# A one-core trunk with experts: a limit on how many expert weight loads are under way

## The chip, the cores and the metric

The kernel runs on one core of one Trainium2 chip. The metric is the device time of one execution in microseconds (us); lower is better. The core has engines with instruction queues of their own: PE (matrix products, with its weight loads shown as PEld), DVE, ACT, POOL, and SP, which here does nothing but wait and issue DMAs. The core's 16 DMA engines move all data between HBM and the on-chip memory.

## The reference

Two layers of a decoder trunk over 288 tokens (256 prompt tokens and 8 sequences of 4 tokens), width 1024, all in float32. Each layer is a token mixer (three recurrent branches) and a feed-forward part. The second layer's feed-forward part is what matters here: eight experts, of which each token takes the two with the highest router logits.

```python
def swiglu(h, w1, w3, w2):
    return (jax.nn.silu(h @ w1) * (h @ w3)) @ w2

def moe_swiglu(h, router, w1, w3, w2):
    logits = (h @ router).astype(jnp.float32)
    top_v, top_i = lax.top_k(logits, TOP_K)
    probs = jax.nn.softmax(top_v, axis=-1)
    gate = jnp.sum(jax.nn.one_hot(top_i, N_EXPERTS, dtype=jnp.float32) * probs[..., None], axis=-2)
    out = jnp.zeros(h.shape, jnp.float32)
    for e in range(N_EXPERTS):
        out = out + gate[..., e:e + 1] * swiglu(h, w1[e], w3[e], w2[e]).astype(jnp.float32)
    return out.astype(h.dtype)
```

w1 and w3 are 1024 x 2816 for each expert, w2 is 2816 x 1024.

## The kernel before

The program does layer 0 (mixer and dense feed-forward), then the mixer of layer 1, then the experts (function `experts`, L2489). Weights never stay on the chip: they come as **slabs** of 128 x 1024 float32, 512 KB each. An expert has 66 slabs (`EX_SLABS`): 44 for w1 and w3 in turn (`UP_SLABS`), 22 for w2. One **pass** is one expert's work on the tokens gathered for it: 88 columns of tokens in the first two passes, then 80, 80, 76, 76 and 72, 72. With these inputs there are eight passes.

PE does a pass in `expert` (L2674): 44 times `up` (L2621; its matmuls are L2630), then the gathering for the next pass (L2602, L2608), then eight times `down` (L2642; matmuls L2650) with the adding of the result to the tokens (`add_up` L2665, `to_tokens` L2672) between. PE's two halves of a weight block are separate matmuls, and the trace has 32 matmul records for a slab, each with a weight load beside it. The passes are loops of PE's own queue (`pe.Fori`), two passes to a loop, with the pass's code written out once in each.

The slabs land in a **ring of 22 places** (`EX_RING`), made of buffers whose data is no longer needed: 2 places in lora_w, 2 in hT, 2 in y_ret, 6 in proj, 8 in ring, 2 in merged, used in this order. Slab n of a pass takes place n % 22, and as 66 is three times 22 each pass begins at place 0. Two neighbouring places are a pair and share a semaphore (`pair_in`); a load adds 16 to it when it has landed. PE waits in `pair_here` (L2613) for both slabs of a pair before it uses the first. After a slab's last matmul PE adds 1 to `slab_done`.

SP issues the loads in the order of use. The first 22 are issued during the mixer's end (`ahead`, L2170). All others go through `load` (L2533): SP waits until `slab_done` says that the slab 22 places earlier has been used (L2534), and issues the load (L2535). Slabs 22 to 65 of the first pass are written out (L2537); the seven further passes are a loop of SP, which reads the expert's number from memory at its start (L2542) and then issues 66 loads (L2543). Nothing else limits how many loads are under way at a time: it is whatever PE's pace of freeing places makes it.

`settle` is an increment of a semaphore that nobody waits for.

Of the kernel before, what the change touches and what calls it, by code (L numbers as in the profile page):

```python
# [55 lines left out]
EX_RING = 22  # L56
# [7 lines left out]
STREAM = ((3, 8), (GLA_H, 6), (GLA_H, 6), (KT, 4), (2, 8), (1, 8))  # L64
# [23 lines left out]
def fills(p, place):  # L88

    return sum(g for g, n in STREAM[:p] if place < n)  # L90
# [8 lines left out]
EX_SLABS = UP_SLABS + EX_DOWN  # L99
# [125 lines left out]
def build(nc, xT_in, w_mix, w_lora, w_rank, w_gkup, vec_in, vecf_in, router_in, w_ff, s_ret, s_gla, s_rw,  # L225
# [50 lines left out]
    def settle(eng):  # L276


        eng.sem_inc(settled, 1)
# [81 lines left out]
    def slabs_in(buffer, n):  # L361
# [3 lines left out]
    EX_AT_LORA, EX_AT_HT, EX_AT_Y, EX_AT_PROJ, EX_AT_RING, EX_AT_MERGED = 0, 2, 4, 6, 12, 20  # L365
    pair_in = {s: slab_in[s - EX_AT_RING] if EX_AT_RING <= s < EX_AT_MERGED else nc.alloc_semaphore(name=f"pair_in{s}")
               for s in range(0, EX_RING, 2)}
# [14 lines left out]
    def slabs_before(layer, p):  # L382

        return layer * (MIX_SLABS + FF_SLABS) + BASE[p]

    def fills_before(layer, s):

        return layer * (fills(len(STREAM), s) + len(range(s, FF_SLABS, RING)))
# [241 lines left out]
    def half(ap, h):  # L630
        return ap[64 * h:64 * h + 64]
# [737 lines left out]
    def rwkv(nc, block, sig, layer, joined):  # L1369
# [33 lines left out]
            "p (g s) -> p g s", g=2)[:, :, 0:GT]  # L1403
        TILES = (0, 0), (1, 1), (0, 1), (1, 0)
        nlev = len(LEVELS64) - 1
# [18 lines left out]
        def group(g):  # L1424
            return slice(NP + GT * g, NP + GT * g + GT)

        def window(g, first=0):
            return slice(NP + GT * g - first, NP + GT * g - first + CH)
# [31 lines left out]
        def _(pe):  # L1460
# [37 lines left out]
            def scores(i):  # L1498
# [6 lines left out]
                for n, src in enumerate((bt, kt)):  # L1505
                    for cp in range(2):
                        for h, r in TILES:
                            c = 2 * cp + r
# [4 lines left out]
            def scores_rest(i):  # L1513
# [5 lines left out]
                for cp in range(2):  # L1519
                    for h, r in TILES:  # L1520
                        c = 2 * cp + r
                        mm(unit(half(BY_HEAD2[h], 1 - r), cp), unit(half(at_rt, h)[:, 0], c), unit(half(bt, h), c),
                           start=True, stop=True)
                for cp in range(2):
                    for h, r in TILES:
                        c = 2 * cp + r
                        mm(unit(half(BY_HEAD3[h], 1 - r), cp), unit(half(bt, h), c), unit(half(at_rt, h)[:, 0], c),
                           start=True, stop=True)
                for h, g in TILES:
                    mm(half(BY_HEAD2[h], 1 - g)[:, 2 * CH:2 * CH + GT], half(at_rt, h)[:, 0, window(g)],  # L1530
                       half(bt, h)[:, group(g)], start=True, stop=True)
                for h, g in TILES:
                    mm(half(BY_HEAD3[h], 1 - g)[:, 2 * CH:2 * CH + GT], half(bt, h)[:, window(g)],
# [955 lines left out]
    def experts(nc, block, sig, layer, merge, rs):  # L2489
# [24 lines left out]
        OTOK, ADD = (bank[6], bank[4]), (bank[7], bank[5])  # L2514
        FF0 = slabs_before(layer, len(STREAM))
        TILES = ((0, 128), (128, 128), (256, 32))

        def passes(eng):
            eng.wait_ge(sig("ctl"), 1)
            return eng.value_load(ctl[0:1, ENTRIES:ENTRIES + 1], min_val=NE - FIXED, max_val=MAXR)  # L2520

        def count(p, per, k):

            i, done = p
            return i * per + (done * per + k)
# [4 lines left out]

        @block.sync
        def _(sp):
            def load(p, e, n):  # L2533
                sp.wait_ge(slab_done, count(p, EX_SLABS, FF0 + n - EX_RING + 1))  # L2534
                sp.dma_start(ex_slot[n % EX_RING], w_ff[e, n]).then_inc(pair_in[n % EX_RING // 2 * 2], 16)  # L2535

            for n in range(EX_RING, EX_SLABS):  # L2537
                load((0, 0), 1, n)
            sp.wait_ge(sig("ctl"), 1)
            after_first = sp.value_load(ctl[0:1, ENTRIES + 1:ENTRIES + 2], min_val=NE - 1, max_val=FIXED - 1 + MAXR)  # L2540
            with sp.Fori(0, after_first) as i:
                e = sp.value_load(ctl[0:1, bass.ds(i, 1)], min_val=0, max_val=NE)  # L2542
                for n in range(EX_SLABS):  # L2543
                    load((i, 1), e, n)
            for k in range(0, KT, 2):
                sp.wait_ge(sig("normed"), k + 2)
                sp.dma_start(yT_out[:, k:k + 2, :], hT[:, k:k + 2, :]).then_inc(sig("stored"), 16)
            sp.wait_ge(sig("stored"), 4 * 16)
# [646 lines left out]
    for layer in range(DEPTH):  # L3195
        with phase(nc, f"in{layer}") as (block, projected):
            project_in(nc, block, projected, layer)
            retained = Signals(nc, f"ret{layer}")
            retention(nc, block, retained, layer, projected)
            gated_linear(nc, block, Signals(nc, f"gla{layer}"), layer, retained)  # L3200
        with phase(nc, f"rw{layer}") as (block, delta):
            joined = Signals(nc, f"join{layer}")
            rwkv(nc, block, delta, layer, joined)
            merge = Signals(nc, f"mix{layer}")
            rs = mix_out(nc, block, merge, layer, delta, joined)
            if layer > 0:
                experts(nc, block, Signals(nc, "moe"), layer, merge, rs)
# [98 lines left out]
```

## Time and profile before

| what | us |
|---|---|
| median of 3 runs (lowest, highest) | 2607.95 (2605.93, 2608.48) |
| the profiled execution, its own time | 2606.82 |
| its span, first to last instruction | 2605.0 |
| the eight passes of the experts, within the span | 1769 to 2590 |

The span is 1.8 us shorter than the profiled execution's own time, and that execution is 1.1 us below the median. A page of the profile gives the busy time of each engine and the share of the DMA engines in 40 slices of the span; the experts are the last 13 of them. From there one goes to the table by stretches (one row a pass), to who waited for whom, to PE's and SP's own instructions in order of time, and to the DMA queues with the time from a load's issue to its landing. In the timelines a row gathers neighbouring instructions of one kind: start, length, engine, line, what is written and read, count, and in brackets the idle time before it with what ended it. "issue" there means that the engine waited for nothing that the profile shows.

### The profile page before, as it was taken

How to read it: one execution, taken by the hardware profiler on the slowest of the kernel's cores; microseconds unless marked ns; L12 is line 12 of the kernel's file. 1: busy time of each engine (PE TensorE's matmuls, PEld its weight loads, DVE VectorE, ACT ScalarE, POOL GpSimd, SP SyncE). 2: the span in 40 equal slices, each digit the busy share in tenths (PEclk: the TensorE clock that was granted, in tenths of full speed). 3: DMA queues.
4: the chain of work that ended last, by engine and by line, in shares of the span. 5: the costliest groups of instructions: out<-in, count | busy, mean ns of one | idle time of the engine just before them, and what ended most of it. 6: DMA issues, size and time to landing. Idle time of an engine off the chain costs nothing. (4 is left out here: it accounts for less than half of the span.)

```text
span 2605.0 us, 103336 instructions
## 1 busy us (share of the span) xinstructions
PE 2437.4 (94%) x45930; PEld 2038.3 (78%) x45930; DVE 1287.5 (49%) x3333; ACT 606.7 (23%) x1798; POOL 0.2 (0%) x4
## 2 busy tenths in 40 slices
PE   9999999999999999999999999999899888878878
PEld 8987666666889998987666666788888787777767
DVE  7666666666786766666666666773111111111111
ACT  2233323333211102233333343211111101111101
POOL 0000000000000000000000000000000000000000
PEclk9999999999999999999999999999999999999989
DMA  6334432222334443334433222367899899999984
GB/s 240 107 139 162 157 131 81 76 76 86 133 131 153 176 147 119 136 131 156 151 122 97 76 80 81 132 238 299 289 348 353 327 355 339 345 340 347 340 301 158
DMA packets 142766, 498.59 MB, mean 191 GB/s; under 512 B 18401, under 2 KB 23137, under 8 KB 139905
## 3 DMA queue, kind: packets, MB, share of 16 engines
q1 hardware_dynamic: 142336, 492.24, 52.5%
q8 instruction: 346, 5.67, 0.8%
q14 instruction: 84, 0.68, 0.1%
HBM read 471.88 MB, written 20.29 MB: 189 GB/s over the span
## 5 line engine op out<-in xcount | busy, mean ns | idle before, releaser
L305 PE MATMUL psum<-hT,ring 128*64 128x144 f32 (+1 forms) x4568 | 457.0, 345 | 3.9 <-DVE hT L2450 1.7
L305 PEld LDWEIGHTS psum<-hT,ring 128*64 128x64 f32 x4568 | 291.7, 137 | 97.7 <-issue 12.2
L2952 DVE TENSOR_TENSOR work<-psum,work 128x88 f32<-128x88 f32 (+3 forms) x176 | 42.4, 241 | 459.5 <-PE psum L2630 459.3
L2630 PE MATMUL psum<-work,ring 128*64 128x88 f32 (+3 forms) x4096 | 157.2, 237 | 35.7 <-issue 35.5
L1782 ACT ACTIVATE work<-psum 128x256 f32<-128x256 f32 (+4 forms) x320 | 103.9, 362 | 349.9 <-PE psum L1693 84.8
L2630 PEld LDWEIGHTS psum<-work,ring 128*64 128x64 f32 x4096 | 151.6, 141 | 39.8 <-issue 39.8
L305 PE MATMUL psum<-work 128*64 128x144 f32 (+4 forms) x2096 | 154.8, 282 | 4.3 <-DVE work L1273 3.6
L305 PE MATMUL psum<-y_ret,work 128*64 128x144 f32 x2400 | 156.2, 286 | 1.2 <-DVE y_ret L546 1.2
L2734 ACT ACTIVATE work<-psum 128x88 f32<-128x88 f32 (+3 forms) x176 | 41.7, 237 | 472.4 <-PE psum L2630 468.8
L305 PEld LDWEIGHTS psum<-y_ret,work 128*64 128x64 f32 x2400 | 148.7, 137 | 1.4 <-issue 1.4
L305 PEld LDWEIGHTS psum<-work 128*64 128x64 f32 (+2 forms) x2096 | 122.0, 136 | 30.7 <-issue 11.4
L2943 DVE TENSOR_TENSOR xT<-xT,psum 128x288 f32<-128x288 f32 x64 | 29.1, 454 | 231.9 <-PE psum L2665 230.9
L2630 PE MATMUL psum<-work,proj 128*64 128x88 f32 (+3 forms) x3072 | 113.8, 231 | 22.2 <-issue 22.1
L305 PE MATMUL psum<-y_ret,ring 128*64 128x144 f32 (+1 forms) x1280 | 127.2, 332 | 2.5 <-ACT work L1782 2.5
L2630 PEld LDWEIGHTS psum<-work,proj 128*64 128x64 f32 x3072 | 109.3, 136 | 25.1 <-issue 25.1
L305 PEld LDWEIGHTS psum<-y_ret,ring 128*64 128x64 f32 x1280 | 79.9, 137 | 18.4 <-ACT work L1782 4.5
L2650 PE MATMUL psum<-work,ring 128*64 128x88 f32 (+3 forms) x2048 | 76.3, 231 | 8.3 <-issue 8.3
L2650 PEld LDWEIGHTS psum<-work,ring 128*64 128x64 f32 x2048 | 72.8, 136 | 11.2 <-issue 11.2
L327 PE MATMUL psum<-hT,ring 128*128 128x288 f32 x252 | 72.8, 408 | 0.0
L2630 PE MATMUL psum<-work,lora_w 128*64 128x88 f32 (+3 forms) x1024 | 46.6, 254 | 27.7 <-issue 27.6
L1578 PEld LDWEIGHTS psum<-work 64*64 64x64 f32 x1408 | 47.3, 134 | 29.4 <-issue 17.7
L305 PE MATMUL psum<-hT,work 128*64 128x144 f32 x928 | 69.1, 287 | 0.0
(538 smaller groups left out, 4389.7 us busy)
## 6 DMA issues: line engine op xcount, KB each, us to landing
ring<-w_mix_dram SPq DMA_DIRECT2D x256, 512.0 KB, 4.1
ring<-w_ff_dram SPq DMA_DIRECT2D x256, 512.0 KB, 5.3
proj<-w_ff_dram SPq DMA_DIRECT2D x144, 512.0 KB, 6.2
lora_w<-w_ff_dram SPq DMA_DIRECT2D x48, 512.0 KB, 4.7
hT<-w_ff_dram SPq DMA_DIRECT2D x48, 512.0 KB, 5.7
y_ret<-w_ff_dram SPq DMA_DIRECT2D x48, 512.0 KB, 6.3
merged<-w_ff_dram SPq DMA_DIRECT2D x48, 512.0 KB, 5.7
work<-s_gla_dram SPq DMA_DIRECT2D x8, 1024.0 KB, 5.1
```

Source lines behind the costliest of these rows:

```text
L305: last = nc.tensor.matmul(out[64 * c:64 * c + 64], weights[:, 64 * c:64 * c + 64], x, start=start, stop=stop)
L327: mm = (in_halves if self.narrow else nc.tensor.matmul)(out, ring[:, s, k, :], rhs[:, k, :], start=(k == 0), stop=(k == KT - 1))
L1578: last = mm(unit(half(W, r), c), half(AT, 1 - r)[:, c], half(X, 1 - r)[:, c], start=True, stop=True)
L1782: return nc.scalar.activation(out, in_, func, **kw)
L2630: last = mm(bank[n % 4][64 * h:64 * h + 64, 0:cap], ex_slot[n % EX_RING][:, k, 64 * h:64 * h + 64], hg[:, k, 0:cap], start=(k == 0), stop= ...
L2650: last = mm(DOWN[m % 2][64 * h:64 * h + 64, 0:cap], ex_slot[(UP_SLABS + n) % EX_RING][:, k, 64 * h:64 * h + 64], hid[:, f, 0:cap], start=( ...
L2734: ac(act1[:, f % 2, 0:cap], bank[2 * f % 4][:, 0:cap], ACT.Silu).then_inc(sig("w1_free"), 1)
L2943: tt(xT[:, k, :], xT[:, k, :], ADD[m % 2][:, 0:T], ALU.add).then_inc(sig("added"), 1)
L2952: tt(hid[:, f, 0:cap], bank[(2 * f + 1) % 4][:, 0:cap], act1[:, f % 2, 0:cap], ALU.mult).then_inc(sig("w3_free"), 1)
```

## The change

`load` gets one more wait ahead of its old one. For the first slab of each pair SP now waits until both slabs of the pair two ahead of it have landed: slab n waits for slabs n - 4 and n - 3 (`UNDER_WAY` is 4). In the loop the first two pairs of a pass wait for the last two pairs of the pass before. The new function `landed` works out the semaphore and its value as `pair_here` does for PE. When a pair is issued, only the pair ahead of it may be under way, so after the second slab's issue there are four at most, and three after the first slab's. Ahead of every load SP also executes one `settle`. The old wait on `slab_done`, the order of the loads, the places, and every instruction of the other engines stay as they are.

```diff
@@ -2514,6 +2514,7 @@
         TILES = ((0, 128), (128, 128), (256, 32))
+        UNDER_WAY = 4
@@ -2530,7 +2531,21 @@
         @block.sync
         def _(sp):
+            def landed(p, n):
+
+                s = n % EX_RING
+                earlier = 0
+                if EX_AT_RING <= s < EX_AT_MERGED:
+                    earlier = fills_before(layer, s - EX_AT_RING) + fills(len(STREAM), s - EX_AT_RING)
+                sp.wait_ge(pair_in[s], count(p, EX_SLABS // EX_RING * 32, earlier * 16 + (n // EX_RING + 1) * 32))
+
             def load(p, e, n):
+                i, done = p
+                if n % 2 == 0 and n >= UNDER_WAY:
+                    landed(p, n - UNDER_WAY)
+                elif n % 2 == 0 and done:
+                    landed((i, done - 1), n - UNDER_WAY + EX_SLABS)
+                settle(sp)
                 sp.wait_ge(slab_done, count(p, EX_SLABS, FF0 + n - EX_RING + 1))
                 sp.dma_start(ex_slot[n % EX_RING], w_ff[e, n]).then_inc(pair_in[n % EX_RING // 2 * 2], 16)
```

What stands in SP's queue before, in the written-out part of the first pass, is below, with the semaphores that each group of loads waits for (`slab_done` alone):

```order
L2535 DMA ring<-w_ff_dram 128x1024 [waits slab_done] x8
L2535 DMA merged<-w_ff_dram 128x1024 [waits slab_done] x2
L2535 DMA lora_w<-w_ff_dram 128x1024 [waits slab_done] x2
L2535 DMA hT<-w_ff_dram 128x1024 [waits slab_done] x2
L2535 DMA y_ret<-w_ff_dram 128x1024 [waits slab_done] x2
```

In the changed kernel the same place of SP's queue reads so (the line of the load is now L2550; pair_in8 and pair_in10 are the last pairs of proj, slab_in0 to slab_in6 the four pairs of ring):

```order
L2550 DMA ring<-w_ff_dram 128x1024 [waits pair_in8,slab_done]
L2550 DMA ring<-w_ff_dram 128x1024 [waits slab_done]
L2550 DMA ring<-w_ff_dram 128x1024 [waits pair_in10,slab_done]
L2550 DMA ring<-w_ff_dram 128x1024 [waits slab_done]
L2550 DMA ring<-w_ff_dram 128x1024 [waits slab_in0,slab_done]
L2550 DMA ring<-w_ff_dram 128x1024 [waits slab_done]
L2550 DMA ring<-w_ff_dram 128x1024 [waits slab_in2,slab_done]
L2550 DMA ring<-w_ff_dram 128x1024 [waits slab_done]
L2550 DMA merged<-w_ff_dram 128x1024 [waits slab_in4,slab_done]
L2550 DMA merged<-w_ff_dram 128x1024 [waits slab_done]
```

No load has moved; every second one has a second semaphore to wait for.

## Rows read from the trace of the kernel before

**Rows 1.** The page: engines' busy time, and DMA share in 40 slices.
```profile
PE 2437.4 (94%) x45930; PEld 2038.3 (78%) x45930; DVE 1287.5 (49%) x3333; ACT 606.7 (23%) x1798; POOL 0.2 (0%) x4
...
DMA  6334432222334443334433222367899899999984
```

**Rows 2.** Table by stretches, five of the eight passes; columns in the first line.
```profile
core 0: us, PE busy (x) PEld busy (x) DVE busy (x) ACT busy (x) POOL busy (x), PEclk, DMA share, GB/s
1769.00:1874.00 105.00, 93.97 (x2243) 88.55 (x2243) 20.20 (x82) 11.96 (x41) 0.00 (x0) 0.99 0.90 333
...
2181.00:2287.00 106.00, 82.64 (x2243) 77.57 (x2243) 13.23 (x43) 13.37 (x44) 0.00 (x0) 0.99 0.92 343
2287.00:2386.00 99.00, 83.12 (x2248) 78.25 (x2245) 12.96 (x42) 10.37 (x40) 0.00 (x0) 0.99 0.92 342
...
2493.00:2590.00 97.00, 82.65 (x2227) 78.40 (x2225) 11.70 (x39) 9.79 (x38) 0.00 (x0) 0.92 0.65 241
```

**Rows 3.** Who waited for whom, 1769 to 2590: total us, times, longest.
```profile
PE psum L2630 <- issue: 106.7, 69, 5.7
...
PE psum L2650 <- issue: 16.3, 22, 2.1
```

**Rows 4.** PE's timeline, from the second pass.
```profile
1917.29 6.91 PE L2630 MATMUL psum<-work,proj 128*64 128x88 f32 x174 [1.49 <-issue]
...
1928.16 5.07 PE L2630 MATMUL psum<-work,ring 128*64 128x88 f32 x126 [0.89 <-issue]
1934.17 2.22 PE L2630 MATMUL psum<-work,ring 128*64 128x88 f32 x52 [0.93 <-issue]
1936.16 2.68 PE L2630 MATMUL psum<-work,merged 128*64 128x88 f32 x64
```

**Rows 5.** SP's queue, 1700 to 2600: what its waits ended on.
```profile
SPq L2535 <- PE psum L2630: 356.5, 348, 16.6
SPq L2535 <- PE psum L2650: 115.0, 123, 3.6
```

**Rows 6.** SP's timeline: the first loads of L2535.
```profile
1770.96 1.56 SPq L2535 DMA_DIRECT2D lora_w<-w_ff_dram  x2
```

**Rows 7.** SP's timeline, some loads of the second pass.
```profile
1906.46 1.56 SPq L2535 DMA_DIRECT2D merged<-w_ff_dram  x2
...
1937.81 1.84 SPq L2535 DMA_DIRECT2D merged<-w_ff_dram  x2
1946.04 1.49 SPq L2535 DMA_DIRECT2D lora_w<-w_ff_dram  x2
1947.82 0.91 SPq L2535 DMA_DIRECT2D hT<-w_ff_dram  x2
```

**Rows 8.** Queues, and issues with median us to landing, 1769 to 2590.
```profile
q8 instruction: 149, 2.44, 1.1%
...
ring<-w_ff_dram SPq DMA_DIRECT2D x184, 512.0 KB, 5.6
proj<-w_ff_dram SPq DMA_DIRECT2D x138, 512.0 KB, 6.2
lora_w<-w_ff_dram SPq DMA_DIRECT2D x46, 512.0 KB, 4.6
```

**Rows 9.** Loads of L2535, 1800 to 2500.
```profile
DMA to landing us min/median/max: 3.1/5.7/8.8
```

**Rows 10.** A stretch of dense loading; columns as in rows 2.
```profile
1950.00:2000.00 50.00, 46.98 (x1131) 43.52 (x1129) 8.12 (x23) 6.94 (x25) 0.00 (x0) 1.00 0.97 354
```

**Rows 11.** DMA, 1887 to 1901.
```profile
DMA packets 1498, 5.48 MB, mean 391 GB/s; under 512 B 168, under 2 KB 168, under 8 KB 1495
```

**Rows 12.** PE's timeline at the end of the last pass.
```profile
2570.65 5.17 PE L2650 MATMUL psum<-work,proj 128*64 128x72 f32 x160
...
2587.61 2.17 PE L2650 MATMUL psum<-work,merged 128*64 128x72 f32 x64
```

**Rows 13.** DMA queues, 2562 to 2590.
```profile
q8 instruction: 7, 0.11, 1.7%
```

## The prediction, written before the changed kernel ran

> **What bounds the kernel now.** I read the page first. PE is busy 94% of the span, and the DMA engines, a third to half busy before, are at nine tenths in the last third, where the experts are [rows 1]. The change touches only that part, so I split it by passes. A pass takes 97 to 107 us, and DMA is at 0.90 to 0.92 of its time until the last pass, whose loads end early [rows 2]. PE's busy time falls with the token columns, from 94 us (88 columns) to 83 (76 and 72), yet the passes hardly get shorter. So something paces PE. The list of waits shows it: PE's matmuls waited 106.7 us (69 times) in `up` and 16.3 us (22 times) in `down`, for "issue", nothing that the profile names [rows 3]. That is 123 us in 91 waits, 1.35 us each. Every other engine's long waits are for PE.
>
> Are these waits for weights? No. SP's waits all end on PE's `slab_done` [rows 5]: each load is issued as soon as its place is free. The pair issued into merged at 1906.5 [rows 7] lands some 6 us later (the median is 5.7 [rows 9]), and PE first reads those places at 1936.2 [rows 4]. Weights lie 24 us ahead of PE.
>
> The waits come after about 127 matmuls or a multiple of it: 1917.29 begins 174 of one group, another 79 follow in ring (253 in all, a wait at 1928.16), then 126, then a wait [rows 4]. 127 matmuls with their 127 weight loads are about 256 instructions. Queue q8 fetched 149 packets of instructions, 2.44 MB, so 16 KB each, in these 821 us: one in 5.5 us [rows 8]. So I take the waits for **PE waiting for its own instructions**, which come over the DMA engines that carry the weights. The end of the last pass supports it: with no load left, q8 still brings 7 packets in 28 us [rows 13], one in 4 us, and PE does 160 matmuls in 5.17 us without a wait [rows 12], 4.1 us for 128. With loads under way a fetch must take longer than the 4.1 to 5.1 us that 126 to 128 matmuls last.
>
> So two clocks run. PE's side: its work and the fetches, which get slower with what is queued for DMA. The supply side: 506 loads (184 + 138 + 4 x 46 [rows 8]), one in 1.57 us over the 794 us from 1771 [rows 6] to about 2565. Now the supply is slaved to PE; loads under way are 5.7 / 1.57 = 3.6 on average.
>
> **The change, part by part.** *The new wait.* It holds SP, whose queue has nothing but the following loads behind it; PE is the one who would wait, and only once the 24 us of lead are used up. Peaks go: two loads can be issued within 0.6 us (0.91 us for two whose own issue is 0.33 [rows 7]), and the longest landing, 8.8 us, against 3.1 for the shortest [rows 9], means several loads ahead; now never more than three. On average I expect 3.2 under way in place of 3.6 (four after a pair's issue, two before the next).
>
> *What PE gains.* A fetch at 1928 took 5.1 + 0.9 = 6.0 us from one wait's end to the next [rows 4]; without loads it takes at most 4.1 [rows 12]. That is at least (6.0 - 4.1) / 3.6 = 0.5 us for each load under way. 0.4 loads less and no peaks: I take 0.4 us off each of the 91 waits, 36 us. Bounds: 0.15 us (14 us), if only the average counts and less than linearly, and 0.6 us (55 us), if the peaks make the waits. PE's side alone then ends the span at 2605 - 36 = 2569, between 2550 and 2591.
>
> *What the supply can do.* Two pairs go per round trip of a pair: if SP reacts in 0.3 us and the second load is issued 0.6 us behind the first, a median landing of 5.7 us makes a round of 6.6 us for four loads, 1.65 us each. That bound assumes that landings do not get shorter, though they now queue behind fewer. With 5.4 it is 1.575. From below the engines bound it: 391 GB/s in a dense stretch [rows 11] is 524288 B / 391 = 1.34 us a load; the shortest landing, 3.1 us, would allow less than that. I take the row of a long dense stretch, share 0.97 and 354 GB/s [rows 10]: 1.48 us. At the start of SP's loop body there is a hole (1939.65 to 1946.04, 6.4 us [rows 7], where a pair is due each 3.0): 3.4 us lost, seven times, 24 us. Last issue: 1771 + 506 x 1.48 + 24 = 2544. It lands 4.8 us later, at 2549; PE needs 2.2 us for its pair and 15.2 us more to the span's end (2589.8 to 2605.0 [rows 12]): 2566. So the lead of 24 us is spent in the course of the passes, and both sides end near each other. The later one, 2569, and 1 us for where they meet give 2570.
>
> *`settle` and the wait themselves.* An increment on a queue that waits for PE or for landings anyway; SP issues no faster than one load in 0.6 us when it may and needs one in 1.48, so they cost nothing while that cover of 0.9 us holds. If SP's longer code made its hole at the loop's start 1 us longer, it would be 7 us in all.
>
> *The other engines.* Nothing moves. DVE and ACT follow PE.
>
> **A rule against it.** What the trace shows is a fetch of 6.0 us beside loads, 4.1 at most without [rows 4, 12]. The Trainium skill, "DMA: Bandwidth & Descriptors", in "Queues, rings and completion order", says that each DMA engine goes round its queues packet by packet. By that rule an instruction fetch waits for a packet or so of the weights, not for all that is queued, and 3 or 6 loads under way are the same to it; that is rival A. By my reading of the rows it waits for the backlog.
>
> **The rivals.**
> *A. The depth does not matter.* Fetches are slow because the engines are busy at all, at 0.90 and more [rows 2]. Then PE keeps its pace of 5.5 us a fetch and the supply, at less than 1.57 us a load, stays slaved to PE. For it: the demand stays the same. Against it: landings spread from 3.1 to 8.8 us, so queues do matter to whatever lies in them. Time: as before, 2607.
> *B. The supply starves PE (slower).* If a load takes more than 1.56 us with this limit, the lead runs out and PE waits at `pair_here`. The price: 506 us for each us of the load's time. At 1.65, the sum above with unchanged landings, the last issue is 1771 + 835 + 24 = 2630, the end 2652, plus 2 for the time outside the span: 2654. At 1.575 it is 2592 + 22 = 2614, or 2616. It decides from 1.557 us a load, where the sum 1771 + 24 + 22.2 + 506 x (the last landing, PE's pair and the tail are the 22.2) gives 2605. For it: the median landing. Against: that median includes queueing behind up to six loads, which the limit removes, and DMA had stretches of 391 GB/s.
> *C. The limit seldom holds.* SP would find the pair landed. With landings of 5.7 us and issues each 1.23 to 1.5 us the pair two ahead is normally still under way at an issue, so I give it little: 2607.
>
> **How the numbers follow.** The forecast (both sides improve, 2550 to 2600): 0.54. A and C: 0.16, within a few us of 2607; of that I count 0.02 as faster, 0.11 as the same and 0.03 as slower. B: 0.30; about half of it lies at loads of 1.555 to 1.58 us, that is 2604 to 2617 (0.03 of it no different from now), the rest above. The span of 2570 with 1.8 us outside it is 2572, and the median lies 1.1 us above the profiled execution: 2573. The low end is PE's best bound, 2550. The high end is 2622, between B's two prices, which leaves out some 0.15 above and 0.05 below. Faster than 2602.7, which is 0.2%, about what a measurement of this kernel can tell from no change: 0.54 + 0.02 = 0.56. Within 0.2%: 0.11 + 0.03 = 0.14. Slower: 0.03 + 0.27 = 0.30.
>
> **What would show it.** Right: PE's waits for "issue" in `up` fall from 1.5 us each to about 1.1, to some 85 us in all; the median landing falls to about 5 us and the longest below 7; SP's waits end on landings; the lead of loads over PE shrinks to a few us in the last passes, and DMA's share is no lower. A shows as the old waits with a new landing median. B shows as PE's matmuls waiting with landings as their releasers, at the first slab of a pair, and a DMA share that falls below 0.85. Wrong altogether would be the guess on the instructions: then the 91 waits stay whatever the landings do.

## The result: slower by 0.6%

| | us |
|---|---|
| changed kernel, median of 3 runs (lowest, highest) | 2624.77 (2620.37, 2627.01) |
| kernel before, the same | 2607.95 (2605.93, 2608.48) |
| ratio, 95% interval | 1.0064 (1.0041 to 1.0086) |
| the changed kernel's profiled span | 2623.0 |

The forecast was 2573, in a range of 2550 to 2622. Rival B of the prediction had it: the supply of weights starves PE.

SP's queue first. Who ended its waits, 1700 to 2620, with total us, times and longest (L279 is the line of the increment that follows the new wait, L2550 the load):

```profile
SPq L279 <- DMA ring<-w_ff_dram: 162.7, 91, 4.2
SPq L279 <- DMA proj<-w_ff_dram: 134.1, 69, 3.5
SPq L279 <- DMA hT<-w_ff_dram: 44.4, 23, 4.4
SPq L279 <- DMA y_ret<-w_ff_dram: 43.6, 23, 3.5
SPq L279 <- DMA merged<-w_ff_dram: 42.9, 22, 4.1
SPq L279 <- DMA lora_w<-w_ff_dram: 40.2, 23, 3.3
...
SPq L2550 <- PE psum L2645: 21.5, 15, 13.8
```

Before, all 471 waits ended on PE's `slab_done` [rows 5]. Now 251 end on landings, and 506 loads are 253 pairs: the limit holds at practically every pair, and the ring's free places no longer say anything. SP's timeline shows the beat that results (start, length, then the issue):

```profile
1915.28 0.99 SPq L2550 DMA_DIRECT2D merged<-w_ff_dram  x2
1918.85 0.99 SPq L2550 DMA_DIRECT2D lora_w<-w_ff_dram  x2
1922.48 0.99 SPq L2550 DMA_DIRECT2D hT<-w_ff_dram  x2
1925.99 0.99 SPq L2550 DMA_DIRECT2D y_ret<-w_ff_dram  x2
...
1950.64 0.99 SPq L2550 DMA_DIRECT2D merged<-w_ff_dram  x2
1953.97 1.00 SPq L2550 DMA_DIRECT2D lora_w<-w_ff_dram  x2
...
2597.03 1.84 SPq L2550 DMA_DIRECT2D merged<-w_ff_dram  x2
```

The 506 loads are issued from 1773.0 to 2597.7: 1.63 us a load, where before (1771.0 to 2560.4) it was 1.56 with the issues slaved to PE. A single load lands sooner, over 1800 to 2520:

```profile
DMA to landing us min/median/max: 3.4/4.9/8.5
```

against a median of 5.7 [rows 9]. But the next pair is not issued on a single load's landing. It waits for a whole pair. From the issues and landings of the trace, a pair takes 6.26 us from its first issue to its second landing (mean): the second load is issued 0.65 us behind the first and lands 5.6 us after its own issue, the first one 4.4 us after its own. SP reacts in 0.28 us, and two pairs go per round: (6.26 + 0.28) / 4 = 1.635 us a load.

The first seven passes of the changed kernel (the columns are in the first line):

```profile
core 0: us, PE busy (x) PEld busy (x) DVE busy (x) ACT busy (x) POOL busy (x), PEclk, DMA share, GB/s
1772.00:1875.00 103.00, 92.47 (x2233) 87.97 (x2231) 19.35 (x76) 11.96 (x41) 0.00 (x0) 1.00 0.89 317
1875.00:1974.00 99.00, 94.85 (x2245) 90.46 (x2245) 13.57 (x42) 10.63 (x40) 0.00 (x0) 0.95 0.91 323
1974.00:2072.00 98.00, 84.57 (x2231) 79.23 (x2227) 13.09 (x41) 13.08 (x43) 0.00 (x0) 0.98 0.91 323
2072.00:2175.00 103.00, 90.38 (x2237) 83.49 (x2239) 13.13 (x42) 10.40 (x40) 0.00 (x0) 0.97 0.90 326
2175.00:2288.00 113.00, 85.22 (x2235) 77.43 (x2235) 12.87 (x41) 13.01 (x43) 0.00 (x0) 1.00 0.89 318
2288.00:2393.00 105.00, 87.13 (x2235) 81.12 (x2235) 12.96 (x42) 10.37 (x40) 0.00 (x0) 0.96 0.90 323
2393.00:2506.00 113.00, 84.70 (x2241) 77.33 (x2243) 12.63 (x41) 12.85 (x42) 0.00 (x0) 0.97 0.91 324
```

Put beside [rows 2] and the passes between them, there are two halves. The first three passes take 300.5 us where before they took 311.8: 11 us **faster**. The other five take 535.3 where it was 508.5: 27 us **slower**. With 2 us more before the first pass and 0.5 us at the end that is the 18 us between the spans.

The turn comes where the lead is gone. The lead is the time from a pair's landing to PE's first use of it. In steps of 22 slabs, at the places in merged, it is in us:

```text
before:   22 28 30 23 27 25 21 27 29 24 26 26 22 26 28 21 26 23 24 26 31 23 22
changed:  15 20 21 12 14  9  0  0  3  0  0  0  0  0  0  0  0  0  0  0  1  0  2
```

Three of these numbers are a pass; the first pass has two, as its first 22 slabs were issued ahead. From the end of the third pass on the lead is zero but for a few us here and there, and PE waits for weights, as the list of its waits over 1773 to 2608 says:

```profile
PE psum L2645 <- issue: 51.6, 31, 6.3
PE psum L2645 <- DMA ring<-w_ff_dram: 24.3, 24, 3.1
PE psum L2645 <- DMA proj<-w_ff_dram: 13.3, 14, 2.6
PE psum L2645 <- DMA merged<-w_ff_dram: 7.6, 7, 2.6
PE psum L2665 <- issue: 7.5, 10, 1.7
PE psum L2665 <- DMA ring<-w_ff_dram: 6.4, 7, 1.9
```

(L2645 and L2665 are the matmuls of `up` and `down`, L2630 and L2650 before.) The waits for "issue" halve, from 123 us [rows 3] to 59. Waits for landings, which did not exist, take their place with some 70 us, counting the smaller rows. Together the waits are 7 us longer than before; PE's busy time is 12 us longer (2449.0 against 2437.4 [rows 1]), 8 of them within the eight passes. PE's weight loads that wait beside running matmuls can be in it, and so can the granted clock of 0.988 in place of 0.990; how the 12 us divide is not measured. One stretch of the sixth pass shows the pattern, a wait at every other pair or so, each ended by a landing:

```profile
2339.17 2.33 PE L2645 MATMUL psum<-work,ring 128*64 128x76 f32 x64 [1.72 <-DMA ring<-w_ff_dram]
2341.66 2.33 PE L2645 MATMUL psum<-work,ring 128*64 128x76 f32 x64 [0.16 <-DMA ring<-w_ff_dram]
2345.49 2.33 PE L2645 MATMUL psum<-work,ring 128*64 128x76 f32 x64 [1.51 <-DMA ring<-w_ff_dram]
2348.00 2.33 PE L2645 MATMUL psum<-work,ring 128*64 128x76 f32 x64 [0.17 <-DMA ring<-w_ff_dram]
2352.90 2.33 PE L2645 MATMUL psum<-work,merged 128*64 128x76 f32 x64 [2.58 <-DMA merged<-w_ff_dram]
```

### The profile page after: what moved, and what is told of

It is laid out like the page before. It is cut to its first block and busy times, and to the rows that moved or that the text cites. A ratio compares the mean times of both kernels' runs of the same rounds, so it can differ in the third digit from the quotient of the medians.

```text
span 2623.0 us, 103933 instructions
## 1 busy us (share of the span) xinstructions
PE 2449.0 (93%) x45930; PEld 2043.3 (78%) x45930; DVE 1287.2 (49%) x3333; ACT 606.8 (23%) x1798; POOL 0.2 (0%) x4
## 5 line engine op out<-in xcount | busy, mean ns | idle before, releaser
L2645 PE MATMUL psum<-work,ring 128*64 128x88 f32 (+3 forms) x4096 | 154.2, 234 | 36.6 <-DMA ring<-w_ff_dram 24.3
L2645 PEld LDWEIGHTS psum<-work,ring 128*64 128x64 f32 x4096 | 147.6, 138 | 42.2 <-issue 42.2
L2645 PE MATMUL psum<-work,proj 128*64 128x88 f32 (+3 forms) x3072 | 116.9, 235 | 22.3 <-DMA proj<-w_ff_dram 13.3
L2645 PEld LDWEIGHTS psum<-work,proj 128*64 128x64 f32 x3072 | 112.1, 139 | 26.0 <-issue 25.9
L2665 PE MATMUL psum<-work,ring 128*64 128x88 f32 (+3 forms) x2048 | 76.1, 232 | 8.4 <-DMA ring<-w_ff_dram 6.4
L2665 PEld LDWEIGHTS psum<-work,ring 128*64 128x64 f32 x2048 | 72.3, 136 | 11.7 <-DMA ring<-w_ff_dram 8.2
L2645 PE MATMUL psum<-work,lora_w 128*64 128x88 f32 (+3 forms) x1024 | 47.0, 258 | 29.9 <-issue 25.6
L2645 PEld LDWEIGHTS psum<-work,lora_w 128*64 128x64 f32 x1024 | 44.1, 158 | 33.0 <-issue 33.0
```

Of the source, the lines that this page charges most:

```text
L2645: last = mm(bank[n % 4][64 * h:64 * h + 64, 0:cap], ex_slot[n % EX_RING][:, k, 64 * h:64 * h + 64], hg[:, k, 0:cap], start=(k == 0), stop= ...
L2665: last = mm(DOWN[m % 2][64 * h:64 * h + 64, 0:cap], ex_slot[(UP_SLABS + n) % EX_RING][:, k, 64 * h:64 * h + 64], hid[:, f, 0:cap], start=( ...
```

## The experiments

Theory T: the limit sets the supply at two pairs per round trip, 1.63 us a load, PE wants less, and the lead of 24 us is spent in about three passes; after that PE runs at the pace of the supply. Beside it stands theory I of the prediction: PE's waits for "issue" are instruction fetches that the weights on the DMA engines hold up. Rivals were that SP's added instructions cost, and that any wait on a landing costs. Times are medians, the ratios are to the kernel before on the same chip; e4, e6, e7 and e8 ran once each.

### Is it the increment, or any limit?

In e1 the waits go and the increment ahead of every load stays:

```diff
-                if n % 2 == 0 and n >= UNDER_WAY:
-                    landed(p, n - UNDER_WAY)
-                elif n % 2 == 0 and done:
-                    landed((i, done - 1), n - UNDER_WAY + EX_SLABS)
                 settle(sp)
```

> The changed kernel without the waits on landings; the added increment ahead of every load stays. Theory T (four under way are too few: a pair's round trip sets the supply at 1.63 us a load): the increment costs nothing, the kernel is back at the time of before, 2605 to 2611 us, median landing 5.7 us. Rival S (SP's added instructions slow its issues): most of the loss stays, 2618 us or more.

2601.48 us, ratio 0.9980 (0.9968 to 0.9993). The loss is gone; rival S falls. The time lies under the expected 2605 to 2611: that the increment alone would make the kernel 0.2% faster was not expected, and I have no explanation for it. It matters below as a yardstick.

In e2 and e3 the limit stays and is wider, six and eight:

```diff
-        UNDER_WAY = 4
+        UNDER_WAY = 6
```

> UNDER_WAY 6: a pair waits for the pair three ahead, five or six loads under way at most. Theory T: three pairs for each round trip of some 7 us give 1.17 us a load, more than the DMA engines can do, so the supply is no longer the limit; the wait holds SP only at the peaks. The time is that of before or a little less, 2595 to 2608 us, landings 5.5 us in the median and none above 8. Rival L (any wait on a landing costs, by SP's reaction and by stopping the stream): slower than before, 2613 us or more.

2601.69 us, ratio 0.9985 (0.9974 to 0.9997), landings 3.1/5.7/8.2 from 1800 to 2500 (shortest, median, longest; a little over the expected 8).

> UNDER_WAY 8: seven or eight at most. Before had rarely more than six under way, so theory T says 2603 to 2610 us, no different from before. Rival L (any wait on a landing costs): 2613 us or more.

2603.21 us, ratio 0.9998 (0.9985 to 1.0010). In e3 SP waited for a landing only once, so it says nothing of such waits; it is in effect e1 again, and the 0.9980 there beside the 0.9998 here shows how far two such ratios can lie apart. In e2 SP waited for landings 74 times, 49 us in all, and the kernel was no slower: a wait on a landing costs nothing by itself, and rival L falls. Nor does cutting the peaks help: with six, 3 loads of 449 took over 7.5 us to land, before 19 of 443, and PE's waits were the same as with the increment alone. Two rows each of PE's waits, 1769 to 2610, of e1 (L2641, L2661) and then of e2:

```profile
PE psum L2641 <- issue: 101.0, 68, 5.9
PE psum L2661 <- issue: 15.2, 18, 1.9
```

```profile
PE psum L2645 <- issue: 101.8, 71, 5.8
PE psum L2665 <- issue: 15.2, 19, 1.7
```

### Does the round trip set the supply?

e4 sets `UNDER_WAY` to 2, so that one pair is under way at a time.

> UNDER_WAY 2: a pair waits for the pair ahead of it, so one pair under way. Theory T: the supply is one pair in a round trip of some 4.6 us (3.1 us shortest landing, 0.65 us for the second issue, 0.3 us reaction, 0.5 us for the queue) or 2.3 us a load: 506 loads take 1164 us instead of 825, the kernel 2960 us, between 2900 and 3050. Rival B2 (the engines' rate, not the round trip, limits the changed kernel): much less than proportional, under 2750 us. Waits of PE for instructions: if they come from the loads queued, those outside the waits for loads fall to a few us in all.

3191.68 us, so rival B2, the engines' rate, falls. Its SP timeline:

```profile
2004.64 0.99 SPq L2550 DMA_DIRECT2D merged<-w_ff_dram  x2
2010.09 0.99 SPq L2550 DMA_DIRECT2D lora_w<-w_ff_dram  x2
2015.72 0.99 SPq L2550 DMA_DIRECT2D hT<-w_ff_dram  x2
2021.52 0.99 SPq L2550 DMA_DIRECT2D y_ret<-w_ff_dram  x2
```

A pair each 5.54 us in the mean, which is the pair's round trip in this run, 5.26 us, and the reaction of 0.28: 2.77 us a load. The law holds in both kernels: pairs allowed, divided by a pair's round trip and SP's reaction. I had the round trip itself too short (4.6 us), by taking a landing of 3.1 us for both loads; so the time missed the expected 2900 to 3050. Waits for "issue" in `up` were 17.3 us in all here, more than the few us expected, beside 491 us of waits for landings.

e5 moves the wait from the pair's first load to its second, so that five are under way at the peak and a round is one load's landing instead of a pair's:

```diff
-                if n % 2 == 0 and n >= UNDER_WAY:
+                if n % 2 == 1 and n >= UNDER_WAY:
                     landed(p, n - UNDER_WAY)
-                elif n % 2 == 0 and done:
+                elif n % 2 == 1 and done:
```

with `UNDER_WAY = 5`.

> The wait stands ahead of a pair's second load, on the pair two ahead of it: four loads under way after that load, five after the next pair's first. Four loads now go per round trip of one load (about 5.2 us and 0.3 us reaction) in place of a pair's (6.5 us). Theory T (the round trip over four loads sets the supply): 1.38 us a load, below PE's need of 1.55, so PE no longer waits for loads and the time is 2598 to 2610 us. Rival (the engines' rate falls with any limit): PE still waits for landings, 2613 us or more.

2602.61 us, ratio 0.9991 (0.9979 to 1.0002). One more load under way, and PE waits for no landing any more, while SP still waits for 72 landings in ring and 69 in proj. The threshold lies between four by pairs and this limit of five. The median landing was 5.4 us and PE's waits for "issue" 115.8 us (97.8 in `up`, 18.0 in `down`), much as in e1.

### Are the waits for "issue" fetches held up by the weights?

e6 and e7 are the kernel before with smaller loads: half and an eighth of each slab. They leave out the rest of the weights, and PE multiplies with what lies there; its instructions are the same.

```diff
-                sp.dma_start(ex_slot[n % EX_RING], w_ff[e, n]).then_inc(pair_in[n % EX_RING // 2 * 2], 16)
+                sp.dma_start(ex_slot[n % EX_RING][:, 0:4], w_ff[e, n][:, 0:4]).then_inc(pair_in[n % EX_RING // 2 * 2], 16)
```

(`0:1` in e7.)

> The kernel before, in which each load of the experts' loop and of the first pass after its first 22 brings only half of a slab (256 KB), so the products use stale weights in the other half. PE's instructions are the same. Theory I (PE's waits for issue are instruction fetches held up by the weights on the DMA engines): with DMA at half its share the waits of 117 us fall to under 40 us and the time to 2500 to 2540 us. Rival P (the waits belong to PE's own instruction stream whatever DMA does): they stay at 100 us or more, 2590 us or more.

2489.49 us, some 10 us under the expected range. PE's waits for "issue" in `up`, 1769 to 2480, and the landings:

```profile
PE psum L2630 <- issue: 32.1, 27, 4.4
```

```profile
DMA to landing us min/median/max: 2.5/3.3/5.2
```

> As the half loads, but an eighth of a slab (64 KB), so DMA is nearly idle and the products use stale weights for the rest. Theory I: the waits for issue between matmuls are gone but for those at the loop's jumps (four of up to 5 us), under 25 us in all, the time 2485 to 2515 us. Rival P: 100 us of waits or more, 2590 us or more.

2466.98 us, again under the range, and of the waits only seven in `up` are left, four of them over 3 us:

```profile
PE psum L2630 <- issue: 17.2, 7, 3.5
```

With DMA at a fifth of its share the passes at last follow the token columns:

```profile
1769.00:1865.00 96.00, 91.14 (x2236) 87.10 (x2235) 19.98 (x80) 11.95 (x41) 0.00 (x0) 1.00 0.18 49
...
2294.00:2372.00 78.00, 75.13 (x2235) 71.42 (x2235) 12.71 (x42) 12.85 (x42) 0.00 (x0) 0.99 0.22 60
```

PE's waits come from the weights' traffic: in the eight passes its waits for "issue" fell by 107 us, from 124 to 17, and rival P falls. PE had not waited for these weights themselves: they were 24 us early. The kernel as a whole became 138 us shorter (2604.98 - 2466.98, a single run of e7). The other 30 us or so are PE's busy time, 694.6 us in the passes before and 662.4 in e7; theory I does not speak of them, and no run says where they come from (the granted clock over the passes was 0.973 before and 0.982 here).

That the thing held up is the fetch of instructions rests on the spacing of the waits and on queue q8; no run changed the fetches alone. The trace of the kernel before has a stronger sign than the spacing. Of PE's 93 waits for "issue" in the experts (the 91 of `up` and `down` and two in the gathering), 88 ended 1.2 to 1.6 us after the end of a packet of q8. A moment taken at random lies anywhere behind the last such packet: 0.6 to 5.3 us, leaving out a tenth at either end. In the changed kernel it is 38 of 43. So PE runs on when a block of instructions has come; only that the weights delay it in the way theory I says stays an inference.

This also decides rival A of the prediction, that the depth does not matter. Take the end of such a wait as the moment at which the next block is asked for. The next packet of q8 then begins after (medians of the kernel before, number of cases in brackets):

| loads under way | 0 | 1 | 3 | 4 | 5 | 6 |
|---|---|---|---|---|---|---|
| us to the next packet of q8 | 0.7 (4) | 1.1 (5) | 2.7 (17) | 3.4 (53) | 3.7 (10) | 3.9 (3) |

(With two there is one case only, 1.1 us.) In the changed kernel it is 2.3 us with three (26 cases) and 3.3 with four (14). In e10 below, with 7 to 12 loads under way, it was 3.8 us (9 cases). So the depth does matter, against rival A, but mostly up to four loads: above that the fetch comes hardly later. This fits e2 and e3, whose wider limits left PE's waits as they were.

e8 is the changed kernel with half loads, so that limit and supply can be told apart:

> The changed kernel with half of each slab loaded (the products use stale weights in the other half). A pair's round trip falls to about 3.1 to 4 us with reaction, 1.0 us a load or less, below PE's 1.2 to 1.4. Theory T: the limit of four costs nothing here, the same time as the half loads without it within 5 us. Rival W (the wait itself, not the rate of supply, costs): 15 us or more slower than the half loads without it.

2481.57 us, 8 us faster than the half loads without the limit, where within 5 us was expected (one run of each, so the sign is weak; the rival's 15 us slower is out). Landings 2.5/3.3/5.6, no wait for a landing, and 22.8 us of waits for "issue" in `up` instead of 32.1. Where the supply suffices, the limit of four does no harm.

### Does the limit gain anything while the lead lasts?

e9 is the changed kernel again, on the chip of e10.

> The changed kernel as it is, on the same chip as the two that follow. Expected ratio to before 1.006 as in the first measurement, between 1.004 and 1.009.

2626.93 us, ratio 1.0081 (1.0066 to 1.0097). Its first three passes took 304.9 us.

e10 keeps the limit for three passes and then lifts it:

```diff
-            with sp.Fori(0, after_first) as i:
+            with sp.Fori(0, 2) as i:
                 e = sp.value_load(ctl[0:1, bass.ds(i, 1)], min_val=0, max_val=NE)
                 for n in range(EX_SLABS):
                     load((i, 1), e, n)
+            with sp.Fori(2, after_first) as i:
+                e = sp.value_load(ctl[0:1, bass.ds(i, 1)], min_val=0, max_val=NE)
+                for n in range(EX_SLABS):
+                    load((i, 1), e, n, False)
```

(`load` does the two waits only if its last argument is not False.)

> The limit of four holds for the first pass and the next two only; from the fourth pass on loads are issued as before. Theory T with fetches (the limit shortens the instruction fetches at the price of the lead, and loses only once the lead is spent): PE's three passes are 10 us shorter together as in the changed kernel, the lead shrinks by as much or more and then stays, no waits for loads follow: 2592 to 2600 us. Rival (the limit shortens nothing; the early gain in the changed kernel was chance): 2603 to 2612 us.

2606.66 us, ratio 1.0001 (0.9989 to 1.0012): no gain, and a miss, as the time is the rival's. But the rival's reason is wrong too, as the first part came much as the theory said. Passes two to four, columns as above:

```profile
1872.00:1970.00 98.00, 95.50 (x2237) 91.27 (x2237) 13.47 (x41) 10.38 (x39) 0.00 (x0) 0.96 0.91 318
1970.00:2072.00 102.00, 86.50 (x2241) 80.65 (x2241) 13.20 (x43) 13.32 (x44) 0.00 (x0) 0.98 0.94 340
2072.00:2181.00 109.00, 87.69 (x2244) 82.11 (x2242) 13.13 (x42) 10.44 (x40) 0.00 (x0) 0.99 0.96 370
```

The first three passes took 301.4 us, 10 less than before. This is hardly chance: in the one trace of each kernel, with the limit of four on they took 300.5, 304.9 and 301.4 us, in e1, e2, e3, e12, e13 and before, without it or hardly touched by it, 310.6 to 314.9. (e5, with five, had 305.2.) The fourth took 109 where it was 100. The lead tells why: `15 18 19 12 11 3 0 1 14 20 28 25`. When the limit was lifted, some 22 places were free at once, and SP filled them all:

```profile
2065.93 7.93 SPq L2550 DMA_DIRECT2D ring<-w_ff_dram  x8
2074.18 1.90 SPq L2550 DMA_DIRECT2D merged<-w_ff_dram  x2
2076.41 3.17 SPq L2550 DMA_DIRECT2D lora_w<-w_ff_dram  x2
```

From 2072 to 2120 landings took 7.6 to 16.2 us, 12.9 in the median, with up to 13 loads under way. PE's waits for "issue" in the fourth pass were 27.0 us (16 times), 16.8 (14 times) in the same pass before. So the gain of three passes was had by leaving 24 us of lead unrenewed, and while the lead is filled up again PE pays it back in longer waits.

e12 has the limit on the last three passes' loads instead, where nothing comes after that needs the lead (the same edit with the loops split at 4 and the arguments exchanged; e11, meant to be the same, gave no time).

> The limit of four holds only from the sixth pass's loads on (the last three passes), where the full lead of some 24 us stands and no later load needs it. Theory T: the supply under the limit is 1.64 us a load and 3 us of hole a pass, PE wants 1.5 to 1.6, so the lead lasts to about the last of these 198 loads and few waits for landings appear; any gain in fetches is at most 5 us: 2598 to 2608 us. Rival (the limit costs wherever it holds, lead or no lead): a third and more of the change's 18 us, 2612 us or more.

2602.12 us, ratio 0.9991 (0.9979 to 1.0003). Lead from the fifteenth number on: `26 17 14 4 0 0 0 0 0`: 4 us are left at the 88th limited load and nothing at the 110th, where I had expected it to last to about the last of the 198. The sixth and seventh pass took 196 us (before 206), the last 106 (before 97), with PE waiting for landings again, 19.5 us in all. The time is in the expected range, but no gain.

e13 has it on the last pass alone, where the lead should just do.

> The limit of four holds for the last pass's 66 loads only. In the last three passes' run the lead of 24 us lasted for some 75 limited loads, so here it should be spent just as the loads end, with hardly a wait for a landing. Theory T with fetches: PE gains some 4 us in instruction fetches and gives nothing back, 2597 to 2603 us, ratio 0.997 to 0.9995. Rival (what the shorter queue gives PE comes back as waits wherever it is tried): ratio 0.9995 to 1.002.

2598.56 us, ratio 0.9976 (0.9963 to 0.9988); no wait of PE for a landing, and the lead's last numbers are `25 20 12 10`. Its ratio is the lowest at full size. But e1, with the increment and no limit at all, had 0.9980 (0.9968 to 0.9993), and the two intervals nearly coincide. That the last pass's limit is worth anything is not shown.

## Why the prediction was wrong

**What bounds the kernel.** Right, as far as the runs go: weights 24 us ahead, and of PE's 123 us of waits all but 17 caused by the traffic on DMA (e6, e7).

**The supply's price: the step that failed.** "I take the row of a long dense stretch, share 0.97 and 354 GB/s [rows 10]: 1.48 us." Measured: 1.63, which over 506 loads is 76 us. That stretch had up to six loads under way; it says what the engines do when nothing limits the queue, not what they do behind this limit. The text had the right sum beside it and gave it up: a round trip of landing, second issue and reaction, 6.6 us for four loads, 1.65 us. The reason for rejecting it, that landings get shorter when they queue behind fewer, is true of a single load (5.7 to 4.9 us) and nearly useless for the pair. Its second load, issued 0.65 us later with its own first one still under way, took 5.6 us to land: 6.26 us from issue to the pair's landing, where I had 6.3. The break-even of 1.557 us holds the 24 us of holes of the next paragraph; without them the same sum gives 1.604. The changed kernel's 1.63 is above both, and no run tells the two apart.

**The hole.** "24 us" for seven holes at SP's loop start was wrong too. In the changed kernel the step from merged to lora_w, which crosses the loop's start, is 3.3 us (1950.64 to 1953.97), an ordinary beat. Before, SP stood still there because it waited for the first slab of `down`, and PE was busy gathering; an SP that runs behind its free places never meets that wait. So B at 1.65 was priced at 2654, holes and all; without the 24 us the same sum gives 2630, 5 us from what was measured. In the forecast this error of 24 us hid part of the 76.

**What PE gains.** The size looked right while the lead lasted: 11 us in three passes, with 28 waits in them, for my 0.4 us each. That is in part luck. PE's waits for "issue" there fell by 8 us, from 27.5 to 19.5, and they became fewer (28 to 15), not shorter; the rest was mostly busy time. My price of 0.5 us for each load under way took the delay of a fetch as proportional to the loads. The table above has 0.7 us from three to four, but only some 0.2 for each load beyond, so the peaks, on which part of my 0.4 us rested, are worth nothing (e2, e3). And I let the gain go on over eight passes beside a supply that could not follow, and did not see that the spending of the lead was what paid for it (e10, e12).

**The bounds of the range.** The high end, 2622, was cut between the two prices of B; the time lay 3 us above. The row of landings would have justified giving B's own sum as much as the forecast; then the range had to reach its price.

**The signs.** Waits of SP on landings, a median landing of about 5 us, a lead that shrinks, matmuls that wait for landings: seen. Not seen: a longest landing below 7 us (it was 8.5), and waits for "issue" in `up` of about 1.1 us each. They were 51.6 us in 31 waits, 1.7 each: PE met fewer of them where it stood waiting for weights instead: the fifth and seventh pass have 24 and 22 us of waits for landings and only 0.2 and 1.8 for "issue". Nor did the DMA share fall below 0.85, B's sign: it stayed at 0.89 to 0.91 while the rate fell from about 340 to 320 GB/s.

## What to carry to other kernels

In these kernels a limit on transfers under way was a limit on the rate: allowed transfers divided by the round trip from issue to the landing that lets the next one go, reaction included. Work this out from the landings of the trace before anything else, and compare it with the consumer's need; if the unit that is waited for is a pair, the pair's round trip counts, and its second member is issued later and lands later than the first. A reserve of early data, a full ring, hides a short supply for a while, so early stretches that look better prove nothing: see what the reserve is at the end, and what its refilling costs.

## What was not expected of the hardware

The 16 DMA engines were as busy behind the limit (share 0.89 to 0.91) as before (0.89 to 0.93 over the first seven passes) and yet moved less: 317 to 326 GB/s against 327 to 348. In the fourth pass of e10, with its long queue, they moved 370 GB/s at 0.96. A busy share of DMA is no measure of its rate here; with few loads queued the same bytes took more busy time.

With seven eighths of the weights' traffic taken away (e7), PE's waits fell by 107 us although none of them was for weights. Few loads under way would be needed, at full size, to free the fetches: the delay of a fetch falls clearly only below four. But 3.0 on average instead of 3.7 took PE's waits for "issue" in the first three passes only from some 27 to some 19 us, and that supply already starved PE later on.
